# A fused decoder layer on one core: buffers re-homed, two expert-weight loads moved up the queue, and the last expert pair without a dispatch

## What is computed

```python
proj = rmsnorm(x, g_mix) @ w_in          # 1024 -> 7680: q, k, v, pool, q_mem, three gates
o    = rmsnorm(diff_attention(rotary(q), rotary(k), v), g_subln) * 0.8   # 8 heads, causal
g    = sigmoid(gate_logits + b_gates)    # one gate per branch and channel
merged = g[0] * (o @ w_b_attn) + g[1] * (pooling(u) @ w_b_pool) + g[2] * (mem_attention @ w_b_mem)
h    = x + merged @ w_out
...
logits = rmsnorm(h, g_ffn) @ w_router + b_router
# top 4 of 32 experts per token, softmax over the four
act = g * sigmoid(1.702 * g) * (u + 1)   # g, u = clamped xb @ w_gate[e] + b, xb @ w_up[e] + b
y[rows] += (act @ w_down[e] + b_down[e]) * weight
out = h + y
```

## Time and profile before

| | |
|---|---|
| median of 3 runs | 1214.23 us |
| the profiled execution | 1214.63 us, of which 1212.8 us lie between its first and last instruction |
| PE busy | 1169.5 us (96%), 5436 matmuls |
| VectorE, ScalarE, GpSimd busy | 436.5, 260.5, 43.7 us |
| transfers | 460.67 MB, mean 380 GB/s; all but 4 MB on SP's queue |
| mixer | from 0 to 302.4 us |
| experts | from 302.4 us, then about 53.2 us a pair, from some 570 us on 58 to 59 us a pair |
| granted TensorE clock | 0.99 of full |

### The profile page before, as it was taken

How to read it: one execution, slowest core, us unless ns; L and a number is a source line. 1 busy time by engine, 2 the same in 40 slices (tenths; PEclk the granted TensorE clock), 3 DMA queues, 4 the chain that set the end, 5 groups by cost and what they waited for, 6 DMA issues and landing times.

```text
span 1212.8 us, 13717 instructions
## 1 busy us (share of the span) xinstructions
PE 1169.5 (96%) x5436; PEld 581.0 (48%) x5436; DVE 436.5 (36%) x758; ACT 260.5 (21%) x463; POOL 43.7 (4%) x72
## 2 busy tenths in 40 slices
PE   9999999999999999999999999989898989899998
PEld 5888888888434344342434343433333343433342
DVE  5788798665222222222222121212122222221222
ACT  5655477542110110111010001101010101010101
POOL 1321101100000000000000000000000000000000
PEclk9999999999999999999999999999999999999999
DMA  9745645689999999999999999999999999999995
GB/s 384 267 148 185 214 142 186 224 363 394 406 427 431 427 432 432 431 432 431 430 431 430 429 429 432 431 432 431 431 431 432 432 432 431 431 431 431 425 428 232
DMA packets 28172, 460.67 MB, mean 380 GB/s; under 512 B 3216, under 2 KB 3984, under 8 KB 6608
## 3 DMA queue, kind: packets, MB, share of 16 engines
q1 hardware_dynamic: 27008, 456.34, 89.4%
q0 software_dynamic: 960, 3.41, 0.9%
q10 hardware_dynamic: 144, 0.03, 0.0%
HBM read 458.72 MB, written 1.05 MB: 379 GB/s over the span
## 4 chain that ended last, share of the span: by engine, by line
PE 66%; DMA 32%; issue 1%; DVE 1%; POOL 0%; SPq 0%; DVEq 0%; POOLq 0%
DMA experts_ring<-in_w_up 32%; PE bank L1773 25%; PE bank L1483 19%; PE bank L1818 7%; PE bank L1701 5%; PE bank L1761 2%; PE bank L1783 2%; PE bank L1447 1%; PE bank L1476 1%; PE bank L1784 1%; DMA raw<-in_mixer_halves 0%; PE bank L1847 0%; PE bank L1693 0%; PE bank L1602 0%; PE bank L1798 0%
## 5 line engine op out<-in xcount | busy, mean ns | idle before, releaser
L1773 PE MATMUL bank<-experts_ring,region 128*64 128x512 f32 x2048 | 468.4, 608 | 31.9 <-DMA experts_ring<-in_w_gate 21.2
L1773 PEld LDWEIGHTS bank<-experts_ring,region 128*64 128x64 f32 x2048 | 150.2, 139 | 325.5 <-issue 317.5
L1818 PE MATMUL bank<-experts_ring,region 128*64 128x512 f32 x1024 | 228.7, 596 | 2.1 <-DMA experts_ring<-in_w_down 1.9
L1483 PE MATMUL bank<-hi_split,region_split 128*128 128x512 f32 x400 | 151.3, 401 | 0.0
L1818 PEld LDWEIGHTS bank<-experts_ring,region 128*64 128x64 f32 x1024 | 73.6, 137 | 137.6 <-issue 136.4
L1483 PE MATMUL bank<-raw_split,region_split 128*128 128x512 f32 x336 | 130.9, 389 | 0.0
L944 ACT ACTIVATE region<-region 128x512 f32<-128x512 f32 x32 | 20.1, 629 | 452.3 <-DVE region L1409 452.3
L973 DVE TENSOR_TENSOR raw_split<-raw,hi_split 128x2048 fp32r<-128x2048 f32 x42 | 96.1, 2288 | 33.9 <-ACT hi_split L693 33.7
L1417 DVE TENSOR_SCALAR region<-bank 128x512 f32<-128x512 f32 x32 | 22.1, 692 | 236.7 <-PE bank L1784 236.7
L1409 DVE TENSOR_SCALAR region<-bank 128x512 f32<-128x512 f32 x32 | 22.1, 691 | 226.3 <-PE bank L1784 226.3
L1483 PEld LDWEIGHTS bank<-hi_split,region_split 128*128 128x128 f32 x400 | 75.1, 188 | 17.4 <-issue 2.6
(11 more groups left out here) (183 smaller groups left out, 760.2 us busy)
## 6 DMA issues: line engine op xcount, KB each, us to landing
experts_ring<-in_w_gate SPq DMA_DIRECT2D x26, 4096.0 KB, 36.6
experts_ring<-in_w_up SPq DMA_DIRECT2D x26, 4096.0 KB, 38.8
experts_ring<-in_w_down SPq DMA_DIRECT2D x26, 4096.0 KB, 39.2
raw<-in_mixer_halves SPq DMA_DIRECT2D x44, 1024.0 KB, 5.0
experts_ring<-in_w_up SPq DMA_DIRECT2D x10, 2048.0 KB, 11.1
experts_ring<-in_w_down SPq DMA_DIRECT2D x9, 2048.0 KB, 14.2
experts_ring<-in_w_gate SPq DMA_DIRECT2D x8, 2048.0 KB, 23.3
experts_ring<-in_w_gate SPq DMA_DIRECT2D x8, 1024.0 KB, 9.3
```

The lines of the kernel that those rows point to most:

```text
L1483: ins = nc.tensor.matmul(unit_bank(u)[:, :], a[:, k, toks], b[:, cols], start=(k == 0 and m == 0), stop=(k == k_n - 1 and m == 2))
L1773: ins = nc.tensor.matmul(dst[h * SLOTS:(h + 1) * SLOTS, :], XE[:, kk, e * SLOTS:(e + 1) * SLOTS], w[:, k, h * HALF:(h + 1) * HALF], start= ...
L1818: ins = nc.tensor.matmul(bank[(2, 1)[e]][h * SLOTS:(h + 1) * SLOTS, :], AHT[e][:, k, half * SLOTS:(half + 1) * SLOTS], w[:, k, h * HALF:(h ...
```

## The change

1. **New homes.** Merged values move from `region8` to `region6`, the attention gates from `region6` to `region4` (over the values V), the turned merged tile from `region10`/`region1` to `region4`/`region6`, the heads' low outputs from `region2` to `region3`, K is laid by halves, the turned normalised h goes to `region5`. Ring half 2 now lies over `x_low` and `region1`, ring half 9 over `region7` and `region10`. The expert biases land in a part of `con`.
2. **SP's list.** Ring half 4 is loaded after H = 34 once the heads' queries are turned; the attention gate's bias (two loads of 512 KiB) moves from GpSimd's queue to SP behind `pv_done`, then ring half 9, the biases, H = 37, ring half 0, H = 38, ring half 1, H = 39, H = 40, ring half 2.
3. **ACT and DVE** take `add_bias(36)`, `add_bias(37)` and their tanh after the last head instead of before it. GpSimd loads the router weights after unit 43 and clears and seeds `OE` with the down bias after the last unit; `combine` waits for that seed instead of PE's entry.
4. **The last pair** is taken out of the loops on ACT and DVE (which now run 5 times 3 pairs), and neither it on PE, ACT and DVE gathers tokens for a following pair.
5. **The end.** The last half comes in three parts instead of two, and the last combine goes by column half: it waits for ACT's copy first, for DVE's only before the second half.

```diff
@@ SP @@
+                load(H)
+                if H == 2 * PIECES.index("ga1"):
+                    sp.wait_ge(qk_done, HEADS)
+                    load_half(0, 4)
+                if H == 2 * PIECES.index("wba0"):
+                    sp.wait_ge(pv_done, HEADS)
+                    for t in range(NT):
+                        sp.dma_start(G["a"][:, t, :], b_gates[0:D].rearrange("(a n) -> a n", a=1).to_broadcast([P, D])
+                                     ).then_inc(gbias_in[2], 16)
+                    sp.wait_ge(merged, 4)
+                    load_half(0, 9)
+                    biases()
                 if H == 2 * PIECES.index("wba0") + 1:
-                    sp.wait_ge(pv_done, HEADS)
-                    biases()
-                    sp.wait_ge(merged, 4)
                     load_half(0, 0)
-                load(H)
-                if H == 2 * PIECES.index("wba1") + 1:
+                if H == 2 * PIECES.index("wba1"):
                     sp.wait_ge(oT_done, HEADS)
                     load_half(0, 1)
-                if H == 2 * PIECES.index("wo0") + 1:
+                if H == 2 * PIECES.index("wo0"):
                     sp.wait_ge(unit_done, UNIT_OF[("ga1", NT - 1, 0)] + 1)
                     load_half(0, 2)
...
-            sp.wait_ge(mgT_done, 4)
-            load_half(0, 4)
...
-            load_half(0, 9)
...
-                for i in range(2):
-                    part = slice(i * 2048, (i + 1) * 2048)
+                for i, part in enumerate((slice(0, 2048), slice(2048, 3072), slice(3072, 4096))):
@@ PE @@
-                pe.wait_ge(hn_ready, NT)
-                dispatch(it + 1)
+                if more:
+                    pe.wait_ge(hn_ready, NT)
+                    dispatch(it + 1)
...
-                            if g == PER_ROUND - 1 and k == 2:
-                                pe.wait_ge(last_in[PER_PAIR], r * 16 + 16)
+                            if g == PER_ROUND - 1 and k >= 2:
+                                pe.wait_ge(last_in[PER_PAIR + k - 2], r * 16 + 16)
...
-            pair_products(0, 0, PAIRS - 1)
+            pair_products(0, 0, PAIRS - 1, more=False)
...
+            for h in range(2):
+                pe.wait_ge((o_lo, o_hi)[h], last * 2 + 2)
```

More of the change, by code:

```diff
@@ new lines, in pair_copies @@
+            def pair_copies(it, more):
+                for e in range(2):
+                    act.wait_ge(g_read, it * 2 + (e + 1))
+                    nc.scalar.activation(SG, GS, ACT.Sigmoid, scale=ALPHA).then_inc(sig_done, 1)
+                for e in range(2):
+                    act.wait_ge(actT_done, it * 2 + (e + 1))
+                    nc.scalar.activation(AHT[e], bank[(2, 0)[e]][:, :].rearrange("p (j s) -> p j s", j=4),
+                                         ACT.Copy).then_inc(actT_copied, 1)
+                    if e == 0:
+                        act.wait_ge(slots_free, it + 1)
+                        act.wait_ge(comb_done, it * 4 + 4)
+                        nc.scalar.activation(PWT, bank[3][:, 0:SEQ], ACT.Copy).then_inc(wT_copied, 1)
+                        if more:
+                            xe_lower_half(it + 1, it * PER_PAIR + 8)
+                for e in range(2):
+                    act.wait_ge(used, it * PER_PAIR + (10 + 2 * e))
+                    nc.scalar.activation(OE[e * SLOTS:(e + 1) * SLOTS, 0:HALF], bank[(2, 1)[e]][0:SLOTS, :],
+                                         ACT.Copy).then_inc(o_lo, 1)
@@ L960, in _, with round_copies @@
+            def round_copies(first):
+                with act.Fori(0, (PAIRS - 1) // 3) as d:
+                    for s in range(3):
+                        pair_copies(first + d * 3 + s, True)
+                pair_copies(first + (PAIRS - 1), False)
+            round_copies(0)
+            with act.If(n_rounds > 1):
+                with act.Fori(1, n_rounds) as r:
+                    xe_lower_half(r * PAIRS, r * PER_ROUND)
+                    round_copies(r * PAIRS)
         @block.vector
@@ L1240, in _ @@
                     head_weights(h + 1)
-                unit(22 + 2 * h)
+                if h + 1 < HEADS:
+                    unit(22 + 2 * h)
+                else:
+                    lo_after(36)
                 if h:
                     oT_lower(h - 1)
-            unit(37)
+            lo_after(37)
+            add_bias(36)
+            add_bias(37)
             oT_lower(HEADS - 1)
@@ new lines, in round_results @@
+            def round_results(first):
+                with dve.Fori(0, (PAIRS - 1) // 3) as d:
+                    for s in range(3):
+                        pair_results(first + d * 3 + s, d * 3 + s, True)
+                pair_results(first + (PAIRS - 1), PAIRS - 1, False)
+            round_results(0)
+            with dve.If(n_rounds > 1):
+                with dve.Fori(1, n_rounds) as r:
+                    nc.vector.tensor_scalar(RANK, RANK, -float(SLOTS), None, ALU.add).then_inc(rank_ready, 1)
+                    dve.wait_ge(rank_ready, r)
+                    dve.wait_ge(slots_free, r * PAIRS)
+                    for t in range(NT):
+                        expert_slots(0, t)
+                    expert_weights(0)
+                    xe_upper_half(r * PAIRS)
+                    round_results(r * PAIRS)
@@ L1442, in _ @@
+            add_results(n_rounds * (4 * PAIRS), range(4), (6, 7, 0, 2), by_half=True)
         @block.tensor
@@ L1471, in unit_k @@
                     toks = slice(t * P, (t + 1) * P)
+                    at = (slice(None), t, k, slice(None)) if name in ("wo0", "wo1") else (slice(None), k, toks)
                     if H < EARLY:
@@ L1837, in _ @@
                             pair_products(r, d, s)
-                    pair_products(r, 0, PAIRS - 1)
+                    pair_products(r, 0, PAIRS - 1, more=False)
             last = n_rounds * PAIRS
-            pe.wait_ge(o_lo, last * 2 + 2)
-            pe.wait_ge(o_hi, last * 2 + 2)
             pe.wait_ge(wT_copied, last + 1)
-            for j in range(4):
-                t, h = divmod(j, 2)
-                if j < 2:
-                    pe.wait_ge(y_added, last * 4 + (j + 1))
-                nc.tensor.matmul(bank[(6, 7, 0, 2)[j]][:, :], PWT[:, t * P:(t + 1) * P], OE[:, h * HALF:(h + 1) * HALF],
-                                 start=True, stop=True).then_inc(comb_done, 1)
+            for h in range(2):
+                pe.wait_ge((o_lo, o_hi)[h], last * 2 + 2)
+                for t in range(NT):
+                    if h == 0 and t == 0:
+                        pe.wait_ge(y_added, last * 4 + 2)
+                    j = h * NT + t
+                    nc.tensor.matmul(bank[(6, 7, 0, 2)[j]][:, :], PWT[:, t * P:(t + 1) * P], OE[:, h * HALF:(h + 1) * HALF],
+                                     start=True, stop=True).then_inc(comb_done, 1)
 _INS = ["x", "mem", "mixer_halves", "b_gates", "pool_w", "w_router",
```

187 lines of the change are left out of this document (75 added, 112 removed).

## The result

The change takes **1222.78 us** (median of 4 runs, 1221.23 to 1223.87), the kernel before beside it 1214.19 us (4 runs, 1214.01 to 1214.35). The ratio is 1.007, 95% interval 1.0052 to 1.0087: slower by 8.6 us, where +4.7 us was forecast. The profiled execution took 1223.87 us; its span is 1222.0 us, 9.2 us more than before.

A forecast was written before the change was run, and what follows sets the result against it. The weight stream was taken to hang on PE's progress at 394 us. Stall 4.4, clock 1.6, relief -1.0 and end -0.3 gave +4.7 on 1214.2, so 1218.9 us; 8-in-10 range 1212.0 to 1220.8, own range 1216.7 to 1221.5.

The forecast's parts named there:

- The queue ahead of H = 37: SP's queue, mixer: 1 MiB more of gate bias ahead makes H = 37 land 2.4 us later, at 244.2 us.
- The rate behind it: SP's queue from H = 37 to H = 39: 2.5 us per MiB, 6.3 MB in 14.6 us.
- The bound of 332 GB/s: Slow case from H = 37 to H = 39: 6.3 MB take 19.0 us, and PE stalls 8.8 us.
- The stall: PE in units 40 and 42 waits for split mixer halves: 0.6 plus 3.8, together 4.4 us.
- The clock: PE behind the 3.8 us wait: clock at half for a while, 1.6 us, bounds 0 and 1.8.
- Relief of the full ring: Expert stage: the 4 MiB load of 394.4 us finds no queue, -1.0 us; upper bound 1.8, lower 0.
- The last pair and the end: End of the expert stage: 0.1 us from the dropped dispatch, 0.2 from the earlier last combine, together -0.3 us.
- At nothing: Parts held to cost 0, among them the waits of add_bias(36) and (37) for a gate bias there by about 234 us.
- At 394 us the stream hangs on PE's progress: Expert stage: the 4 MiB load waits for PE's products, so each us PE loses in the mixer is lost at the end.
- A: Rival, mixer: halves come in time, stall only 0.7 to 1.1 us, no clock fall, 1214.0 us; chance 0.20.
- B: Rival, first refill: no stall, prefetch keeps 1.8 to 2.6 us, in all -2.5 to -3.3, 1211.3 us; chance 0.12.
- C: Rival, mixer: stall below 2.5 us or a clock that holds, +1 to +3, 1216.5 us; chance 0.16.

The follow-up runs named there:

- the second execution: The change itself, not edited, run again: median 1223.62 us, ratio 1.0061 to the kernel before.
- the first step of the order: The change with every ring half and the biases issued behind the mixer half that had stood behind them: 1218.17 us, ratio 1.0028 to the kernel before.

## Why the prediction was off

**The direction and the mechanism were right**: slower by over 0.2%, by a wait of PE in the middle of units 40 and 42 for H = 37 and H = 39. The time lies 3.9 us above the forecast and 2.0 us above the range. Step by step:

- *The queue ahead of H = 37: mis-sized, and this is the main error.* "H = 37 has 1 MiB of gate bias more ahead: 241.8 + 2.4 = 244.2." It landed at 246.9 and, in the second execution, 245.6. The price of that 1 MiB was 3.8 to 5.1 us. The step took the steady rate for a load that stood first in an idle queue and that reads one row 128 times. The one row is 0.6 to 1.4 us of it. With the bias out of SP's queue H = 37 lands at 243.2, earlier than forecast, though the same bytes had to move; that points to the place of this load at the head of SP's queue. Why a MiB there costs 3.4 us even from 128 rows stays open. The windows from 228 us to the landing of H = 37, before and change, show where to look:

```profile
228.00:241.80 13.80, 13.80 (x66) 11.47 (x65) 4.52 (x5) 4.94 (x11) 2.39 (x4) 1.00 0.84 308
228.00:246.90 18.90, 18.90 (x90) 15.72 (x89) 4.67 (x5) 5.16 (x11) 0.93 (x2) 1.00 0.91 307
```

That is about 4.3 MB before, where 3.4 MB stand in the list up to H = 37, and 5.8 MB in the change, where 4.5 MB do. So bytes of loads behind H = 37 had moved before it was complete, 0.9 MB before and 1.3 MB now. From the one to the other 1.5 MB more went in 5.1 us more, about 300 GB/s. The prediction counted 1.05 MB, at 431.

- *The rate behind it: right.* Ring half and mixer half together took 7.4, 7.3 us. The bound of 332 GB/s for that stretch was not needed.
- *The stall: 4.4 us forecast, 6.6 and 5.9 us measured.* The second wait was right (3.8 against 3.56 and 3.58), because the first had already moved PE's need. The first was forecast at 0.6 us and came at 3.06 and 2.27 us. A late front of a queue is paid once, at the first unit that runs out of margin.
- *The clock: right in size.* Forecast 1.6 us; 4.60 against 3.02 us for the same 12 matmuls. But its source, a fall behind idle stretches of 2.54 and 2.62 us, would have given the measured first wait of 3.06 us the same price, and the clock stayed at 1.00 behind it. That only one wait paid is in part luck. The group also starts about 0.3 us slower when the work before it has run out (3.02 us, against 2.74 us where PE was kept busy beyond the split); the prediction had no term for it.
- *Relief of the full ring, -1.0 us: there is none.* The 4 MiB load of 394.4 was to land in 12.2 us; it took 13.9 us, as before. It was not alone in either kernel: the load before it landed at 398.0, 3.6 us after its issue (406.8 and 3.4 us in the change). The reasoning took the queue ahead of it for ring halves that would now be there in time. They were refills that PE itself had released, and they moved with it. The Trainium skill ("DMA: Bandwidth & Descriptors", section "Anatomy of one DMA — SWDGE (gpsimd) path") would have had 11.6 us; no 4 MiB load here came near that, the shortest took 13.5 us. That section is on transfers that GpSimd starts, and these are started by SyncE.
- *The last pair and the end, -0.3 us: in line with the run that has it alone.*
- *"At nothing", the bias for `add_bias(36)`.* "If that load took 5 us more, PE would feel it": on SP's queue it was there at 235.6, and no wait showed; on GpSimd's it came at 241.6, and PE waited 2.90 us.
- *"At 394 us the stream hangs on PE's progress"*: the consequence holds (6.3 us of PE time, 7.2 us at the end), the place does not. It hangs on PE before about 388 us.

The sum as measured, on the profiled execution: 3.06 + 3.56 of waits, 1.6 of clock, 0.6 of slower starts, nothing from ring and end: 8.8 of the 9.1 us. Of the rest, 0.2 us were there by unit 38 (its start at 234.51 against 234.31), from something earlier that was not traced.

**The rivals.** A (halves in time) and B (prefetch pays) fell with the two waits. B's idea, that the stream keeps what ring half 9 no longer takes ahead of the first refill, can be read from the order with all mixer halves first. It has no wait; ring half 4 goes out at 206.5 and 9 at 231.5 us, far earlier than before (0, 1 and 2 go out 11 to 13 us later than before, at 242.6, 253.5 and 266.5). Its first refill landed after 4.8 us in place of 7.4, its 4 MiB load of 394.1 after 14.5, and it took 1214.79 against 1214.77 us. So a shorter queue at 304 us buys nothing at the end. C (short stall or steady clock) fell too.

**The range** was too narrow by its own bounds: its top, 1220.8, lies below the 1221.5 of the forecast's own range, and the stall's upper bound of 8.8 us was left out on the argument that the steady rate is nearer. The stall came between the two.

No order tried beats both kernels. The best, 1214.79 us, equals the kernel before.

## What to carry to other kernels

On a queue that keeps its order, a prefetch is free only if everything behind it has that much margin. Write down for each load in the list when it is needed, less the steps between landing and use, and put loads with slack of tens of us (here the ring's halves) behind loads with slack of a few (the mixer's), to the very last of them: each half left ahead only handed the delay on to the next. Cost a load at the start of a busy stretch by what such loads took there, not by the steady rate; and before you credit relief somewhere, ask who released the bytes that stand ahead. A kernel whose executions spread over 5 us (1214.76 to 1220.02) while those of its neighbour in the list spread over 2 is worth a search for a margin near zero; a single late execution is not, since the kernel before has one of 1220.13 us too.

## What the runs showed of the hardware

- A load of 1 MiB in two parts, each reading one 4 KiB row 128 times, took 4.9 to 6.5 us from the second issue to landing in eight executions, on a queue that was idle before, against 4.2 us from 128 different rows in one execution. Started on GpSimd's queue while ring half 9 and H = 37 (3 MiB) went over SP's, its second part took 12.3 us: it landed at 241.6, between the 238.0 of the one and the 243.2 of the other. A second queue did not carry it past the first one's bytes.
- When a load in SP's queue was complete, bytes of the loads behind it had moved too: about 0.9 MB when H = 37 landed in the kernel before, about 1.3 MB in the change.
- The granted clock of PE fell behind waits of 3.54, 3.56 and 3.58 us in the mixer (to 0.78, 0.66 and 0.70 over 266 to 271 us) and behind one of 2.35 us (to 0.66 over 273 to 278 us, in the first step of the order), and not behind waits of 1.60, 2.27, 3.06 and 2.90 us there (1.00 in the windows behind). In the expert stage groups of 32 matmuls took 8.62 and 8.78 us behind 2.54 and 2.62 us. So the length of the wait alone does not decide; what else does was not tried. Work without use in the wait, 128x512 matmuls into a bank nobody reads, held the clock at 1.00.
- The same load in the same place landed up to 1.3 us apart in two executions of one kernel (H = 37 at 245.6 and 246.9; 0.6 us of it because it was issued later, at 231.7 and not 231.1). A difference of that size between two single traces is no finding; the pair for the clock could be read only because its landings agreed.
